# Spreading per-row values by transposes in a decoder trunk: attention denominators inverted wide, router weights held stationary

## What is computed

```python
u = rmsnorm(x, norm1_g)
proj = u @ w_in                    # four groups of 4 heads of width 64
# A latent attention, B dilated windows, C forgetting attention, D window of 128 with sinks
#   s = q @ k * dh**-0.5 + bias ;  C adds cum[t] - cum[s], cum = cumsum(log_sigmoid(fg))
#   p = softmax(s) ; D: the denominator also holds exp(sink)
#   out = p @ v
h = x + concat(oa, ob, oc, od) @ w_o
g_prob  = softmax(xt @ w_rg + b_rg)            # 4 groups, best one kept
e_logit = (xt @ w_re + b_re)[group]            # 8 experts in it, best two kept
gate = p_g * top_p / sum(top_p)
y = sum over the two experts of gate * (silu(xb @ w1[e]) * (xb @ w3[e])) @ w2[e]
x = h + y
```

## Time and profile before

| | us |
|---|---|
| median of 3 runs | 2083.46 (2081.15 to 2083.76) |
| profiled execution, its own time | 2083.47 |
| span from first to last instruction | 2081.3 |
| TensorE busy | 1943.8 (93%) |
| VectorE busy | 728.1 (35%) |
| ScalarE busy | 562.0 (27%) |
| GpSimd busy | 309.9 (15%) |
| mean granted TensorE clock | 0.965 |

### The profile page before, as it was taken

How to read it: one execution, slowest core, us unless ns; L and a number is a source line. 1 busy time by engine, 2 the same in 40 slices (tenths; PEclk the granted TensorE clock), 3 DMA queues, 4 the chain that set the end, 5 groups by cost and what they waited for, 6 DMA issues and landing times. The chain is left out here.

```text
span 2081.3 us, 26383 instructions
## 1 busy us (share of the span) xinstructions
PE 1943.8 (93%) x9728; PEld 1132.9 (54%) x9728; DVE 728.1 (35%) x2113; ACT 562.0 (27%) x1321; POOL 309.9 (15%) x356
## 2 busy tenths in 40 slices
PE   7999998999999899999699999899999998999992
PEld 4555556777655544444355555477775555444441
DVE  0111116666444322222212221266664443222214
ACT  1211226655422211111121121456563221111110
POOL 0333330010000111111013333200100001111110
PEclk9999999999999799999899999999999997999996
DMA  7000010020171289999722110000205115999986
GB/s 252 11 21 11 0 51 1 2 82 12 37 293 61 100 331 407 402 404 380 266 81 81 41 51 17 34 2 2 92 2 226 62 51 189 358 405 405 397 325 253
DMA packets 94638, 322.41 MB, mean 155 GB/s; under 512 B 22065, under 2 KB 36017, under 8 KB 78129
## 3 DMA queue, kind: packets, MB, share of 16 engines
q1 hardware_dynamic: 70704, 271.92, 34.1%
q0 software_dynamic: 14400, 33.58, 4.2%
q10 hardware_dynamic: 9408, 15.23, 2.1%
HBM read 296.56 MB, written 42.99 MB: 163 GB/s over the span
## 5 line engine op out<-in xcount | busy, mean ns | idle before, releaser
L426 PE MATMUL banks<-r_win,r_tile 128*128 128x384 f32 (+3 forms) x1536 | 531.0, 505 | 10.6 <-DMA r_win<-in_w_in 8.2
L426 PEld LDWEIGHTS banks<-r_win,r_tile 128*128 128x128 f32 x1536 | 292.5, 192 | 227.7 <-issue 61.5
L1599 PE MATMUL banks<-r_proj,r_tile 128*128 128x512 f32 x512 | 231.3, 597 | 0.0
L1738 PE MATMUL banks<-r_proj 128*128 128x512 f32 x512 | 225.0, 592 | 0.0
L1079 ACT ACTIVATE r_win<-r_win 128x256 f32<-128x256 f32 (+7 forms) x256 | 177.4, 695 | 29.4 <-DVE r_win L1153 21.3
L981 PE MATMUL banks<-r_win 64*128 64x512 f32 (+3 forms) x704 | 134.9, 503 | 20.1 <-DVE r_win L1125 10.8
L1738 PEld LDWEIGHTS banks<-r_proj 128*128 128x128 f32 x512 | 94.8, 190 | 107.1 <-issue 107.1
L1599 PEld LDWEIGHTS banks<-r_proj,r_tile 128*128 128x128 f32 x512 | 93.0, 190 | 95.6 <-issue 95.6
L1738 PE MATMUL banks<-r_win,r_proj 128*64 128x512 f32 (+1 forms) x512 | 134.9, 614 | 8.5 <-DVE r_proj L2038 4.3
L992 PE MATMUL banks<-fixed,r_win 128*128 128x128 f32 x984 | 132.5, 280 | 7.2 <-ACT r_win L1087 7.2
L2083 DVE SCALAR_TENSOR_TENSOR r_proj<-banks,rs,r_proj 128x256 f32<-128x256 f32 x50 | 24.2, 483 | 326.8 <-ACT r_proj L1825 326.8
(11 more groups left out here) (217 smaller groups left out, 2070.0 us busy)
## 6 DMA issues: line engine op xcount, KB each, us to landing
r_win<-in_w SPq DMA_DIRECT2D x96, 1024.0 KB, 14.4
r_proj<-in_w SPq DMA_DIRECT2D x96, 1024.0 KB, 14.9
r_win<-in_w_in SPq DMA_DIRECT2D x6, 1536.0 KB, 20.5
r_proj<-in_w_o SPq DMA_DIRECT2D x2, 4096.0 KB, 13.0
residual<-r_tile ACTq DMA_DIRECT2D x16, 512.0 KB, 2.9
out<-r_tile SPq DMA_DIRECT2D x16, 512.0 KB, 7.4
r_win<-expert_rows SPq DMA_DIRECT2D x16, 512.0 KB, 9.2
r_proj<-expert_rows SPq DMA_DIRECT2D x16, 384.0 KB, 3.7
```

The source lines that it names most:

```text
L426: mm = pe.matmul(bk[b][:, 0:CHUNKS[c]], uT[j][:, k, :], w_ch[c][:, k, :], start=(k == 0), stop=(k == KT - 1))
L1599: mm = pe.matmul(bk[2 * (t % 2) + c][:, :], mix[t][:, k, :], s.w_o[:, k, 512 * c:512 * c + 512], start=(k == 0), stop=(k == KT - 1))
L1738: mm = pe.matmul(bk[2 + j][at, 0:2 * F].rearrange("p (c n) -> p c n", c=2), xT[j][:, k, at], w13[c][:, :, k, :], start=(k == 0), stop=(k = ...
```

## The change

- `plan_ring` and TensorE's order: within a step the spread of the reciprocals comes last, behind the spread of the gates' sums and the heads' transposes.
- `invert`: VectorE writes the reciprocals straight into `r_s`, each one 64 times (4 blocks x 2 heads x 64 = 512 columns), from the denominators read with a broadcast. It first waits for its own earlier `normalise`, which read `r_s`. ScalarE's copy no longer waits for that.
- `spread_norm`: four transposes of 128 columns of `r_s` take the place of eight matmuls.
- `spread_cum`: four transposes of the broadcast sums take the place of four matmuls.
- Router: the weights `w_r` (36 columns) become the stationary side and the tile's transposed h the moving side of 128 columns. Even k go to partitions 0 to 35 of bank 5, odd k to 64 to 99. ScalarE copies both parts to SBUF (`copy_turned`), and after one more part of the projection one matmul with a table of two stacked identities (`both_parts`, written by VectorE at the start of the block) turns them back and adds them (`turn_logits`). TensorE waits for that table at the start of the block and for ScalarE's copy before the turn and before the next tile's transposes.

```diff
@@ plan_ring
-        ring += [("norm", key, "a") for key in norm_at(st)]
         ring += [("cum", key, "v") for key in cum_at(st)]
         ring += [("qk", key, "v") for key in heads_at(st)]
+        ring += [("norm", key, "a") for key in norm_at(st)]
@@ spread_cum
-                mm = pe.matmul(bank[:, t * P:(t + 1) * P], bcast(cum[:, 4 * half + t, h:h + 1], [P, P]),
-                               s.ident[:, :], start=True, stop=True)
+                mm = pe.transpose(bank[:, t * P:(t + 1) * P], bcast(cum[:, 4 * half + t, h:h + 1], [P, P]),
+                                  s.ident[:, :])
@@ spread_norm
-                for j in range(2):
-                    qb = HALF * half + b
-                    mm = pe.matmul(bank[HD * j:HD * (j + 1), b * P:(b + 1) * P],
-                                   bcast(rden[:, pair % 2, j, qb:qb + 1], [P, HD]), s.ident[:, :],
-                                   start=True, stop=True)
+                mm = pe.transpose(bank[:, b * P:(b + 1) * P], r_s[:, b * P:(b + 1) * P], s.ident[:, :])
@@ TensorE, within a step
-            for pair, half in norm_at(st):
-                spread_norm(pair, half)
             for key in cum_at(st):
                 spread_cum(*key)
             for pair, q in heads_at(st):
                 transpose_heads(pair, q)
+            for pair, half in norm_at(st):
+                spread_norm(pair, half)
@@ norm_out (ScalarE)
-            if pair + half > 0:
-                act.wait_ge(g.on.sem, g.on.at(layer, 2 * pair + half))
@@ invert (VectorE)
-            nc.vector.reciprocal(rden[:, x, :, b], den[:, x, :, b]).then_inc(g.rd.sem, 1)
+            n = 2 * pair + half
+            if n > 0:
+                dve.wait_ge(g.on.sem, g.on.at(layer, n))
+            nc.vector.reciprocal(
+                r_s.rearrange("p (b j c) -> p b j c", b=HALF, j=2),
+                bcast(den[:, x, :, b].rearrange("p j b -> p b j").unsqueeze(3), [P, HALF, 2, HD])).then_inc(
+                    g.rd.sem, 1)
@@ router_logits
-                    mm = pe.matmul(bk[6][:, 0:R], hT[t % 2][:, k, :], w_r[:, k, :], start=(k == 0),
-                                   stop=(k == KT - 1))
-                mm.then_inc(g.lm.sem, 1)
+                    part = HD * (k % 2)
+                    mm = pe.matmul(bk[5][part:part + R, 0:P], w_r[:, k, :], hT[t % 2][:, k, :], start=(k < 2),
+                                   stop=(k >= KT - 2))
+                mm.then_inc(g.lt.sem, 1)
+
+            def turn_logits(t):
+                pe.wait_ge(g.lc.sem, g.lc.at(layer, t + 1))
+                pe.matmul(bk[6][:, 0:R], turned[t % 2][0:HD + R, :], both_parts[0:HD + R, :], start=True,
+                          stop=True).then_inc(g.lm.sem, 1)
@@ TensorE, within a tile
                 router_logits(t)
-                more(3, 4)
+                more(3)
+                turn_logits(t)
+                more(4)
@@ ScalarE, within a tile
+            def copy_turned(t):
+                act.wait_ge(g.lt.sem, g.lt.at(layer, t + 1))
+                if t >= 2:
+                    act.wait_ge(g.lm.sem, g.lm.at(layer, t - 1))
+                nc.scalar.activation(turned[t % 2][0:HD + R, :], bk[5][0:HD + R, 0:P], ACT.Copy).then_inc(g.lc.sem, 1)
+
             for t in range(NT):
                 scale(t)
+                copy_turned(t)
                 gate_exps(t)
@@ VectorE, start of the block
+            v.tensor_tensor(both_parts, s.ident[:, 0:R], s.ident[:, HD:HD + R], ALU.add).then_inc(g.bp.sem, 1)
```

More of the change, by code:

```diff
@@ L1327, in route_signals @@
     g.xo = sig("hT_ready", 2 * NT)
+    g.lt = sig("router_logits_turned", NT)
+    g.lc = sig("turned_logits_copied", NT)
     g.lm = sig("router_logits_done", NT)
@@ L1338, in route_signals @@
     g.kr = sig("key_steps", 1)
+    g.bp = sig("turning_table_ready", 1)
     g.rk = sig("rank_steps", RANK_STEPS)
@@ L1435, in route_experts @@
     cnt = take(2)
+    turned = [w[:, a:a + P] for a in (22272, 22272 + P)]
+    both_parts = take(R)
     cnti = take(1, I32)
@@ L1607, in transpose_h @@
                     pe.wait_ge(g.xo.sem, g.xo.at(layer, 2 * t))
+                    pe.wait_ge(g.lc.sem, g.lc.at(layer, t))
                 xs = h_t[t].rearrange("p (q k) -> p k q", k=KT)
@@ L1671, in _ @@
             pe.matmul(bk[7][:, 0:P], s.ident[:, :], bcast(s.junk[:, 0:1], [P, P]), start=True, stop=False)
+            pe.wait_ge(g.bp.sem, g.bp.at(layer, 1))
             s_wo = s.attend_sems.wo
```

## The result

The changed kernel takes 2162.2 us in the median of four runs (2157.1 to 2165.3), the kernel before 2083.6 beside it: a ratio of 1.0378 with a 95% interval of 1.0353 to 1.0402, so 79 us slower (73 to 84). The profiled execution has a span of 2157.9 us, 76.6 more than before. The forecast was 2157, in a range of 2112 to 2205.

The account below looks back on a forecast made before the run. TensorE was taken to bound the kernel, stopping when VectorE is held too long. Stalls less transpose savings +61, half clock +18, router -6, table wait +0.6 gave +74 us on 2083.5: 2157 us, range 2112 to 2205.

Parts of the forecast that it names:

- What bounds: Attention: TensorE sets the time; VectorE, at 64%, stops it when held longer than the slack of one step.
- The length of the reciprocal: VectorE's 512-column reciprocal: 6.4 ns a column, 3.4 us, with 3.1 and 4.2 as ends.
- What stands behind it: Attention: TensorE's spread waits for the reciprocal or a bank behind VectorE's copy; 30.4 us a layer, spread savings included.
- third steps: Third step of a pair, spread's bank behind VectorE's copy: logits 2.4 us late, or 2.0 with gates' sums.
- first steps: First step of a pair, spread's bank emptied by ScalarE: logits 1.55 us late, or 0.9 with gates' sums.
- window steps: Other window steps and the last spread: no transposes fill the wait; 2.8 us late, 4 times a layer.
- The clock: Attention: idle TensorE before the spread falls to half clock in 13 of 32 places, 1.4 us each, +18 us.
- The savings: TensorE work: 16 us at the reciprocals' spreads, 10 at gates' sums, 16 at the router; router net -6.
- The sum: Whole kernel: 61 + 18 - 6 + 0.6 = +74 us on 2083.5 us, 2157 us.
- +61: Attention of both layers: 2 x 30.4 us of later TensorE work, the savings of the transposes already in it.
- (a): Attention: same stalls, but TensorE's clock stays at its upper level; +56, 2139 us; chance 0.16.
- (c): VectorE's reciprocal: cost mostly per instruction, 512 columns about 0.7 us like a copy; 2060 us; chance 0.08.

Follow-up runs that it names:

- the narrow kernel: Changed kernel, but VectorE takes the reciprocal of 8 columns and copies it wide to 512: 2063.15 us, ratio 0.9911 to the kernel before.
- the held one: Kernel before, plus four further VectorE reciprocals of 128 columns behind the narrow one, results read by nobody: 2173.21 us, ratio 1.0424.
- copies-first: Changed kernel, with VectorE's copies of the transposed weights ahead of the wide reciprocal: 2163.97 us, ratio 1.0383 to the kernel before.
- filled kernels: Changed kernel with weight copies ahead of the reciprocal, plus 16 idle transposes or 9 idle matmuls before each spread: 2143.26 and 2142.69 us.
- the router's part: Kernel before with only the router's change (weights stationary, logits turned back): 2075.73 us, ratio 0.9963.

## Why the prediction was right, step by step

- **What bounds.** TensorE's path through the attention, with VectorE 64% busy behind it: borne out by the narrow kernel and by the held one.
- **The length of the reciprocal.** 3.4 us from the slope between 8 and 30 columns; measured 3.35. The next instruction starts 3.26 us after it, against 3.3. Between 128 and 512 columns the slope is (3.35 - 0.94) / 384 = 6.3 ns, against 6.4 from rows 4 to 6. The estimate from the repeat count of 8 in the Trainium skill ("VectorE: DVE Perf Modes", "First, the fixed hardware budget"), 4.3 us, was too long by 0.95.
- **What stands behind it.** Spread at 4.1 and 3.56, measured 3.95 and 3.50. The next logits of third steps 2.4 late, measured 2.3 where the clock stayed up and 2.75 where not; of first steps 1.55, measured 1.50; with gates' sums 0.9, measured 0.8 and 1.0, and 2.0, measured 1.9 and, at half clock, 2.95; in the window steps 2.8, measured 2.7 and 3.1. The prediction took the reason step by step, here the value and there the bank. The copies-first and the held kernel show that which of the two ends a wait is an accident of order, and that the held engine is the cause.
- **The clock.** The mechanism is right and its size was partly a choice. Forecast were 13 places at 1.4 us, +18. The trace has 16 places, at 13 of the longer gaps and 3 of the shorter, where the forecast took 11 and 2. TensorE's busy time is 30 us above the narrow kernel's, so each place costs 1.9 us of it. In time less comes back: the filled kernels are 19 to 21 us faster, since TensorE waits for VectorE for part of what it gains.
- **The savings.** Router -6, measured -7.7 (-11 to -4). Gates' sums -10, measured -6 (-9 to -3): this term was too large. The group's busy time fell by 8.1 us and not by 9.9 (0.163 us a transpose in its place and not 0.135), and 3.4 of it went into waits. The denominators' 128 transposes take 24.5 us, 0.19 each, and not 17.3: 4.5 us of the difference are half clock, as they take 20.0, 0.16 each, in the narrow kernel. The mean of L992, 0.135, is taken over longer rows of transposes too (ten in a row take 1.31 us at 329.88, four take 0.63), so it was too low for rows of four.
- **The sum.** +74 forecast, +79 measured (73 to 84). It is nearer than its terms, and some of that is luck. The forecast's +61 holds 26 us of savings, so it meant 87 us of stalls; TensorE's idle time grew by 75. Against that the half clock was taken too low and the savings too high. The terms can't be parted cleanly, since a TensorE at half clock comes later to its next wait and waits less there.
- **The rivals.** (a) without the clock, 2139 us, is near what the filled kernels give, 2143. (c), a reciprocal as short as a copy, 2060 us, is near what the narrow kernel gives, 2063. Neither is the changed kernel.

What stays open: why some gaps are followed by half clock and others of the same length are not, how much of the gain of the narrow kernel is the denominators', and where the projection's 5 us more in the router's part arise.

## What to carry to other kernels

Price a change by the columns that each instruction works on and what a column costs in that operation, not by the number of instructions: a spread that looks like a free broadcast on the output made a slow operation 64 times as wide. Take the slow operation narrow and spread its result with a copy, which cost 0.43 us here against 3.35. And where two engines hand banks to each other in program order, ask how long the one may be held before the other stops; here 3.35 us on an engine that was busy two thirds of the stage cost 3 us each time (97 us for 32 spreads, half clock included).

## What the runs showed of the hardware

- A VectorE reciprocal costs 6.3 ns a column (0.94 us for 128, 3.35 for 512), a 32-bit copy from SBUF to SBUF 0.43 us for 512, less than a copy of 512 columns from PSUM (0.63 to 0.68). I had expected 0.6 to 0.7 for it.
- Useless work in TensorE's gaps raised the mean clock of the attention from 0.92 to 0.98 and saved 19 to 21 us, as well with transposes as with matmuls.
- Gaps of 1.5 to 3.7 us on TensorE were followed by half clock in 16 of 32 places, the shortest of them 1.74 us; two gaps of 2.51 us had either clock behind them.
- Four 32-bit transposes of 128 columns in a row cost 0.16 us each (20.0 us for 128), where the mean over rows of up to fourteen is 0.135.
- 36 stationary columns in each half of the array, alternating, gave 17.1 us for 256 records of 128 moving columns, 0.067 us each (18.0 and 0.070 with the router's part alone), close to the rate of full halves of 64 in rows 3 (0.066).
